# Three edits in one: shared stacks issued before the guest weights, an index order by fours, and two causal attentions worked in groups of two duos

## The reference, cut to what matters

```
h = rmsnorm(x)
A:   I[t,s] = sum_h w[t,h] * relu(qi[t,h] . ki[s])      # indexer, 8 heads
     keep the 128 best causal keys of each query, softmax over them, times va
B:   softmax(q.k/8 + c[t] - c[s], causal) v             # "forgetting" attention, 8 heads
x  = x + rmsnorm((sig(h Wma) * yA + sig(h Wmb) * yB) Wout), then a gated embedding
even layer: differential attention of 8 heads x 2 maps over 768 keys (256 context, 512 tokens),
            a short convolution, modulation of both layers from (silu(c) w_mod)
odd layer:  neighbourhood attention, Fourier mixing
```

## Time and profile before

| what | value |
|---|---|
| median of 3 runs | 1315.1 us (1314.51 to 1316.66) |
| profiled execution | 1319.82 us, its span 1317.9 us |
| PE busy | 1246.1 us, 95% |
| weight loads of PE | 999.3 us, 76% |
| DVE, ACT, POOL busy | 675.4, 632.7, 463.3 us |
| mean granted TensorE clock | 0.981 of full |
| moved by DMA | 140.33 MB, mean 106 GB/s |

### The profile page before, as it was taken

One profiled execution on the slowest core, in us unless ns is written; L12 is line 12 of the kernel. 1 busy time (PEld: TensorE's weight loads), 2 busy tenths in 40 slices (PEclk: granted clock), 3 DMA queues, 4 the chain that ended last, 5 costly groups with the idle time before them and its releaser, 6 DMA issues. The chain is left out here.

```text
span 1317.9 us, 19569 instructions
## 1 busy us (share of the span) xinstructions
PE 1246.1 (95%) x7148; PEld 999.3 (76%) x7148; DVE 675.4 (51%) x1293; ACT 632.7 (48%) x1355; POOL 463.3 (35%) x360
## 2 busy tenths in 40 slices
PE   7999999999999999899598989999999999999997
PEld 6877777776788788888476767788878788777785
DVE  4676966655315245547173637551834701555353
ACT  7544327654523366623264646552546422655533
POOL 5544434221444455512132323331452323222351
PEclk9999999999999999999798989999999999999999
DMA  6322541101322523501325341221234232221442
GB/s 230 134 72 70 187 160 65 65 33 49 128 97 95 193 96 106 197 1 65 113 94 182 116 168 59 93 75 65 96 112 146 85 115 86 67 94 65 161 133 91
DMA packets 28429, 140.33 MB, mean 106 GB/s; under 512 B 4304, under 2 KB 5712, under 8 KB 15728
## 3 DMA queue, kind: packets, MB, share of 16 engines
q1 hardware_dynamic: 21584, 117.72, 25.5%
q10 hardware_dynamic: 6752, 21.35, 4.9%
HBM read 122.74 MB, written 6.29 MB: 98 GB/s over the span
## 5 line engine op out<-in xcount | busy, mean ns | idle before, releaser
L1255 POOL TENSOR_TENSOR w_low<-w_raw,w_high 128x512 fp32r<-128x512 f32 x256 | 350.5, 1381 | 653.0 <-ACT w_high L1436 652.4
L1436 ACT CAST w_high<-w_raw 128x512 fp32r<-128x512 f32 x256 | 153.9, 621 | 258.5 <-PE psum L660 171.7
L660 PE MATMUL psum<-x_high,w_high 128*128 128x512 f32 x528 | 219.2, 415 | 3.7 <-DVE e_conv L2614 1.0
L660 PE MATMUL psum<-x_high,w_low 128*128 128x512 f32 x528 | 206.6, 391 | 0.0
L660 PE MATMUL psum<-x_low,w_high 128*128 128x512 f32 x528 | 206.2, 391 | 0.0
L660 PEld LDWEIGHTS psum<-x_high,w_high 128*128 128x128 f32 x528 | 99.7, 189 | 32.8 <-issue 10.1
L660 PEld LDWEIGHTS psum<-x_high,w_low 128*128 128x128 f32 x528 | 99.1, 188 | 21.6
L660 PEld LDWEIGHTS psum<-x_low,w_high 128*128 128x128 f32 x528 | 99.6, 189 | 16.6 <-issue 1.0
L2550 DVE TENSOR_REDUCE small<-psum 128x1 f32<-128x768 f32 (+1 forms) x96 | 70.0, 771 | 72.1 <-PE psum L1040 72.1
L660 PE MATMUL psum<-w_high,x_high 128*128 128x512 f32 x224 | 88.4, 395 | 0.9 <-POOL w_low L1255 0.6
L660 PE MATMUL psum<-w_high,x_low 128*128 128x512 f32 x224 | 87.3, 390 | 0.0
(11 more groups left out here) (484 smaller groups left out, 2862.0 us busy)
## 6 DMA issues: line engine op xcount, KB each, us to landing
w_raw<-stream SPq DMA_DIRECT2D x98, 1024.0 KB, 4.9
x_kept<-arena ACTq DMA_DIRECT2D x8, 512.0 KB, 3.7
arena<-x_kept ACTq DMA_DIRECT2D x8, 512.0 KB, 5.6
arena<-bias ACTq DMA_DIRECT2D x8, 512.0 KB, 3.9
q_masked<-e_q_high SPq DMA_DIRECT2D x24, 96.0 KB, 2.5
arena<-x SPq DMA_DIRECT2D x4, 512.0 KB, 5.2
arena<-x ACTq DMA_DIRECT2D x4, 512.0 KB, 5.0
arena<-ctx ACTq DMA_DIRECT2D x4, 512.0 KB, 4.4
```

Source lines behind the costliest of these rows:

```text
L660: mm = pe.matmul(o, l, r, start=(first and n == 0 and kind != "fc"), stop=(last and n == len(passes) - 1))
L1255: pool.tensor_tensor(PLACE[u][1], RAW[:, g % 2, u % 4, :], PLACE[u][0].bitcast(F32), ALU.subtract).then_inc(w_lo, 1)
L1436: act.copy(PLACE[u][0], RAW[:, g % 2, u % 4, :]).then_inc(w_hi, 1)
```

## The change

1. **Stacks and guests.** The stacks may be issued from the granule after `cb_0`'s on, and a modulation's granule counts as free one step later than before. Modulation parts of the even attention are now five, (0,4) to (1,2), after steps 2, 10, 18, 34 and 42, none after 26. Part (1,3) is a guest of `eo0` after its units 1 and 4, and is turned after the first tile of `eo1`. The order in SP's queue becomes: `cb_0`+`ub_0`, stack -1, first half of (0,4), second half, stack 1, `bb_0`+`cb_1`, both halves of (0,5), stack 10, `bb_1`+`ub_1`, first half of (1,0), stack 13 (before: stack -1 behind both halves of (0,4), stack 10 behind the first half of (1,0), stack 23 between the halves of (1,1)). ACT no longer rounds `n_k`'s first two units before the context's last norm.
2. **Index order.** `INDEX_SUMS` goes by groups of four (0, 2, 1, 3, then 4, 6, 5, 7 and so on), `ga`'s gate is multiplied one round of the selection earlier (n == 7 for 8).
3. **Causal attentions.** Every fourth step: transposes of step s-4 and a product piece first, then the values of two duos into one bank, then the scores of two duos into banks 0 to 3; on the other steps only transposes and a product piece. All transposes use bank 4. ACT copies values of two duos at once (16 copies of 256 columns for 32 of 128); exponentials, norms and copies come one step earlier in the lists of ACT and DVE.

```diff
-LATE_HOSTS = ("n_k", "ud")
-EVEN_MODS = [m for m in MODS if m not in MODS[:4] + MODS[10:]]
+GUEST_AT = {"eo0": (1, 4)}
+LATE_HOSTS = ("eo0", "n_k", "ud")
+EVEN_MODS = dict(zip((0, 1, 2, 4, 5), MODS[4:9]))
...
-        INDEX_SUMS = [6 * pr + n for pr in range(HEADS // 2) for n in (0, 2, 1, 3, 4, 5)]
+        INDEX_SUMS = [first + n for first in range(0, len(INDEX), 4) for n in (0, 2, 1, 3)]
...
-                accs = score_pair(keys, (s % 3, (s + 1) % 3), prep_of(name, pr), t, kh, kl, more=name == "b")
+                accs = score_pair(keys, (s % 4, s % 4 + 1), prep_of(name, pr), t, kh, kl, more=name == "b")
...
-                acc = open_bank(key, 3 + s % 2)
+                acc = open_bank(key, 4)
...
-            for s in range(len(BOTH) + 7):
-                if s >= 8 and s % 2 == 0:
-                    values_both((s - 8) // 2)
-                if s < len(BOTH) and s % 2 == 0:
-                    score_both(s)
+            for s in range(len(BOTH) + 5):
                 if 4 <= s < len(BOTH) + 4:
                     turn_both(s - 4)
                 if s < len(BOTH):
                     feed("ab", pieces, 1)
+                if s >= 8 and s % 4 == 0:
+                    values_both(s // 2 - 3)
+                if s < len(BOTH) and s % 4 == 0:
+                    score_both(s)
+                    score_both(s + 2)
...
-            by_tiles("eo1", mixed, gives_back=False)
+            by_tiles("eo1", mixed, lambda t: turn_due(), gives_back=False)
...
-                return min([s for s, mod in MOD_AFTER.items() if mod == granule[1]], default=len(EVEN))
+                return min([s + 1 for s, mod in MOD_AFTER.items() if mod == granule[1]], default=len(EVEN))
...
-                if g >= granule_of(UNITS["cb_1"][-1]):
+                if g > granule_of(UNITS["cb_0"][-1]):
...
-            for s in range(len(BOTH) + 8):
+            for s in range(len(BOTH) + 5):
...
-                if 2 <= s < len(BOTH) + 2:
-                    exps_both(s - 2)
-                if 5 <= s < len(BOTH) + 5:
-                    turned_out(*BOTH[s - 5])
-                if s >= 9 and s % 2:
-                    values_both((s - 9) // 2)
+                if 1 <= s < len(BOTH) + 1:
+                    exps_both(s - 1)
+                if 4 <= s < len(BOTH) + 4:
+                    turned_out(*BOTH[s - 4])
+                if s >= 8 and s % 4 == 0:
+                    values_both(s // 2 - 3)
...
             high(UNITS["eo1"][-1])
             mixed_out(0, range(ST))
+            guest_rows(GUEST["eo0"])
...
-            high(UNITS["n_k"][1])
             rms("x3_c", LT, lambda t: E_O[:, ST + t, :], context_summed, M_JUNK, c=ST, each=True)
...
-                if n == 8:
+                if n == 7:
                     gated("ga", GA)
...
-            for s in range(1, len(BOTH) + 5):
-                maxima_both(s - 1)
-                if 3 <= s < len(BOTH) + 3:
-                    name, i = BOTH[s - 3]
+            for s in range(len(BOTH) + 4):
+                if 2 <= s < len(BOTH) + 2:
+                    name, i = BOTH[s - 2]
                     norm(name)(i, ATT[name].tile(i))
-                if s >= 5:
-                    turned_out(*BOTH[s - 5])
+                maxima_both(s)
+                if s >= 4:
+                    turned_out(*BOTH[s - 4])
```

More of the change, by code:

```diff
@@ L66 @@
 HOSTS = ("ga", "gb", "vb", "mb0")
-LATE_HOSTS = ("n_k", "ud")
-EVEN_MODS = [m for m in MODS if m not in MODS[:4] + MODS[10:]]
-GUEST = {host: mod for host, mod in zip(HOSTS + LATE_HOSTS, MODS[:4] + MODS[10:])}
+LATE_HOSTS = ("eo0", "n_k", "ud")
+EVEN_MODS = dict(zip((0, 1, 2, 4, 5), MODS[4:9]))
+GUEST = {host: mod for host, mod in zip(HOSTS + LATE_HOSTS, MODS[:4] + MODS[9:])}
 UNITS = {}
@@ L84 @@
     _j, _rest = divmod(4 * _b - UNITS[SLIM[0]][0], 4)
-    if 0 <= _j < len(EVEN_MODS):
+    if _j in EVEN_MODS:
         GRANULES += [("m", EVEN_MODS[_j], half) for half in range(2)]
@@ L453, in build @@
         GRANULE_STEPS = 8
-        MOD_AFTER = {GRANULE_STEPS * j + 2: mod for j, mod in enumerate(EVEN_MODS)}
+        MOD_AFTER = {GRANULE_STEPS * j + 2: mod for j, mod in EVEN_MODS.items()}
         TURN_AFTER = {step + 2: mod for step, mod in MOD_AFTER.items() if mod[1] < 4}
         def even_units(s):
-            granules_in = (s - 5) // GRANULE_STEPS + 1
-            return min(fed["e"][2 * s - 1] + ROOM, UNITS[SLIM[0]][0] + 4 * granules_in + 3)
+            in_step, rest = divmod(s - 5, GRANULE_STEPS)
+            known = in_step + 1 if in_step in EVEN_MODS or in_step < 0 else in_step + 2
+            return min(fed["e"][2 * s - 1] + ROOM, UNITS[SLIM[0]][0] + 4 * known + 3)
         N_CONSTS = 3
@@ L771, in gemm @@
                     unit(chunk, k, x, c, part)
-                    if chunk in GUEST and k in (1, 5):
+                    if chunk in GUEST and k in GUEST_AT.get(chunk, (1, 5)):
                         modulate(*GUEST[chunk], int(k > 1))
@@ L920, in values_both @@
                 name, d = BOTH_DUOS[n]
[L921 to L924, removed]
+                if (name, d) == ("b", 1):
                     for kt in range(ST):
@@ L928, in values_both @@
                 acc = open_bank(key, 5)
-                for kt in range(t + 1):
+                for duo in (d - 1, d):
+                    pr, t = ATT[name].duos[duo]
                     for hh in range(2):
[L931 to L934, removed]
+                        consumed(pe, (name, "T", 2 * duo + hh, 0))
+                    own = slice(P * (duo % 2), P * (duo % 2) + P)
+                    for kt in range(t + 1):
+                        for hh in range(2):
+                            head = 2 * pr + hh
+                            v = A_VW[:, kt, 0:64] if name == "a" else A_VB[:, kt, 64 * head:64 * head + 64]
+                            mm = pe.matmul(acc[64 * hh:64 * hh + 64, own], v,
+                                           A_PT[:, 2 * (duo % 2) + hh, P * kt:P * kt + P], start=kt == 0, stop=kt == t)
                 fills_bank(mm, key)
@@ L1574, in _ @@
                 w = P * (t + 1)
-                if n % 6 == 0 and pr + 1 < HEADS // 2:
-                    prep_i(pr + 1)
+                if n % 6 == 0 and n // 6 + 1 < HEADS // 2:
+                    prep_i(n // 6 + 1)
                 if n >= 3:
@@ L1610, in turned_out @@
                 if d >= 2:
-                    filled(act, (name, "O", d - 2))
+                    filled(act, (name, "O", d - 2 | 1))
                 elif name == "b":
-                    filled(act, ("a", "O", len(ATT["a"].duos) - 2 + d))
+                    filled(act, ("a", "O", len(ATT["a"].duos) - 1))
                 n, key = a.keys(a.tile(i)), (name, "T", i, 0)
@@ L1643, in values_both @@
                 q = A_QA if name == "a" else A_QB
-                frees(act.copy(q[:, pr, P * t:P * t + P], ps[:, 0:P]), key)
+                frees(act.copy(q[:, pr, P * (t - 1):P * (t + 1)], ps[:, 0:2 * P]), key)
             def kept_raw(c):
@@ L2299, in gated @@
                     frees(dve.tensor_tensor(g[:, j, :], g[:, j, :], BANK[fills[(c, j)][0]][:, :], ALU.mult), (c, j))
[L2301 to L2304, removed]
             def modulation(layer, parts, rows=None):
@@ L2326, in modulation @@
                         consumed(dve, ("modT", layer, i))
-                    scale_up(layer)
+                    a, b = COL[f"npre{layer}"]
+                    link(dve.scalar_tensor_tensor(MC[:, layer, 8:16, :], MC[:, layer, 8:16, :], 1.0,
+                                                  COLS[:, a:b].unsqueeze(2).broadcast_to((P, 8, 2)), ALU.add, ALU.mult))
             link(dve.tensor_scalar(A_MASK[:, 0:P], square("causal"), -1.0, None, ALU.mult))
@@ L2356, in turned_out @@
                 if d >= 2:
-                    filled(dve, (name, "O", d - 2))
+                    filled(dve, (name, "O", d - 2 | 1))
                 elif name == "b":
-                    filled(dve, ("a", "O", len(ATT["a"].duos) - 2 + d))
+                    filled(dve, ("a", "O", len(ATT["a"].duos) - 1))
                 key = (name, "T", i, 0)
@@ L2395, in _ @@
             modulation(0, (1,))
-            for s in range(1, len(BOTH) + 5):
-                maxima_both(s - 1)
-                if 3 <= s < len(BOTH) + 3:
-                    name, i = BOTH[s - 3]
+            for s in range(len(BOTH) + 4):
+                if 2 <= s < len(BOTH) + 2:
+                    name, i = BOTH[s - 2]
                     norm(name)(i, ATT[name].tile(i))
-                if s >= 5:
-                    turned_out(*BOTH[s - 5])
+                maxima_both(s)
+                if s >= 4:
+                    turned_out(*BOTH[s - 4])
             for c, name, q, g, hi, lo in (("ga", "oa", A_QA, GA, BH, BL), ("gb", "ob", A_QB, GB, CHA, CLA)):
-                for d in range(len(ATT[name[1]].duos)):
+                for d in range(1, len(ATT[name[1]].duos), 2):
                     consumed(dve, (name[1], "O", d))
@@ L2637, in _ @@
```

(8 more changed lines are left out.)

## The result

The changed kernel takes 1296.9 us (median of 4 runs, 1294.9 to 1298.5), the kernel before 1315.9 in the same comparison (1314.5 to 1318.6). The ratio is 0.9845, 95% interval 0.9826 to 0.9864: faster by 19 us. The forecast was 1288, range 1279 to 1302: the direction and the range held, the gain of 27 was 8 too high.

A forecast was written before the change was run, and what follows sets the result against it. PE was taken as the bound, busy 1246.1 of 1317.9 us. Stacks 33.0, `eo1` -3.0, context norm +2.3, index +4.0 and attentions -9.1 sum to 27.2 off the 1315.1 median: 1288, range 1279 to 1302.

The forecast's parts named there:

- Part 1, stacks: Even attention: earlier stacks and no modulation after step 26 remove waits and low clock, 35.5 us, net 33.0.
- Moving (1,3): Even attention after step 26: no modulation left, so 5.85 us of load wait and 2.9 + 0.1 of low clock go.
- `eo1`: First tile of `eo1`: its loads land later and POOL's eight low parts finish late; PE loses about 3.0 us, bounds 0 and 6.
- Context norm: Context's last norm: DVE's two sums get faster, PE's wait shrinks about 1.5 us, half the clock fall counted; +2.3, bounds 0 and 3.6.
- Index: Index scores and `gate_a`: new order frees banks and gates earlier, ending waits of 2.9 and 1.1 us; +4.0, bounds 2.5 and 4.
- Part 3, the attentions: Causal attentions: waits on the single transpose bank's copies outweigh regrouping gains; -9.1 us, bounds -5.6 and -11.5.
- shape changes: Causal attentions: fewer switches between matmul shapes per two duos, saving 3.2 us.
- The single bank costs nothing: Rival, causal attentions: prompt copies remove the waits, so the stage gains 7.6 us; 1271, or 1280 if half vanish; chance 0.15.
- the start isn't freed: Rival, even attention's start: something else holds the stacks, so 18.9 us stay; 1307; chance 0.08.
- The clock falls in the attentions: Rival, causal attentions: short waits lower the clock in every group, 16 x 1.5 = 24 us; 1312, half of them 1300; chance 0.10.
- my term of 3.0 for the low clock there: Even attention, behind the load wait after step 26: 2.9 + 0.1 us of low clock expected to go.

The follow-up runs named there:

- SP's order alone: Kernel before with only the new order of SP's queue, all six modulations staying in the even attention: 1292.5 against 1316.0 us, ratio 0.9804.
- the last experiment: Changed kernel with transposes alternating between banks 4 and 5, plus the first half of a finished `ma` chunk copied one step earlier by ACT: 1275.9 us, ratio 0.9686.
- two banks: Changed kernel with transposes taking turns between banks 4 and 5, a group's values using the one free between: 1276.7 us, ratio 0.9699.
- the copy ahead of the next maximum: Changed kernel with the copy of a transposed block placed before the next maximum in DVE's list instead of behind it: 1290.2 us, ratio 0.9796.
- attentions-alone kernel: Kernel before with only the causal attentions' new order and single transpose bank, stacks and index as before: 1332.9 against 1316.1 us, ratio 1.0122.
- the cut in the kernel before: Kernel before with POOL's low parts of the attention weights cut to 8 of 512 columns; single run, attention stage 122.4 us against 123.6.
- both edits: Changed kernel with transposes in banks 4 and 5 and DVE's copy of a transposed block ahead of the next maximum: 1277.9 us, ratio 0.9700.

## Why the prediction was right, and where it was off

*Part 1, stacks: held.* The text has 26.6 for the waits of the start and of step 13, less 2.5 for new ones: 24.1; SP's order alone measured 23.5. Moving (1,3): 8.85 of wait and low clock less 3.0 at `eo1`, 5.9; measured 4.7. Together 30.0 against 28.2. In the traces the even attention's stretch gained 33.6 and the next one lost 1.9, but the profiled execution of before had more time at a low clock than others (below).

*`eo1`: held.* POOL finishes eight low parts one after the other, and the first tile waits for each of the last five; 1.9 us in the table and 2.3 against the run with (1,3) left in place, for 3.0 forecast.

*Context norm: its mechanism half wrong.* 1.3 us on average in the traces, nothing in the medians, against 2.3. The sums got faster as told; that POOL's part would hit DVE's next low part instead and take back 1.3 of the 1.7 was not foreseen. What is left is about the clock fall behind the wait, of which the prediction counted half.

*Index: held,* 4.0 against 4.0 between the two traces, to the tenth by luck: with the old order the attentions begin at 202.6 to 205.3 us in four traces, with the new one at 198.1 to 199.2 in ten, on average 5.1 earlier. The waits named (2.9 and 1.1) are gone. No run changes the index order alone.

*Part 3, the attentions: the step that failed.* The mechanism was right: the single bank, waits on copies at the transposes, "some 15 to 20 us in all" (15.8 by the profile). The sum of -9.1 with bounds of -5.6 and -11.5 was not: alone it measured -16.8, in the traces -14.5, or -15.4 at the same clock. That is the whole error of the forecast: 9.1 less 17 to 18 is the 8 to 9 us by which the medians missed 1288. The prediction had two workings. By hand: 17.6 + 0.3 + 2.9 of waits, less the 3.5 of old waits and 3.2 of shape changes, is 14.1, close to what the traces show. The walk of both orders through their lists gave 130.7 less 121.5 = 9.2, and I took it although the two differed by 5, and the text gives no reason for the gap. The old order's 121.5 was close to its measured 122.7; the new one's 130.7 was 7.4 short. Two runs say what it left out. DVE's norms take longer beside POOL: 3.4 us of the new stage, and 0.3 of the old one at the same clock. ACT's copies of finished sums hold PE's next product (1.9 us in the last experiment, with two banks; by start-to-start times some 0.7 with one, which no run of its own shows). The rest, about 3 us, stays open.

The start-to-start times show how large the waits are. A transpose behind a product starts 0.232 us after it when nothing waits. In the old order 30 of these take 7.3 us, so 0.3 of wait; in the new one 46 take 31.7, so 21.0 of wait, where the waits view shows 15.8: it counts idle time only from the modelled end of the product. With two banks the same 46 take 12.1.

The order without its waits seems to have saved more than the 3.2 put down for shape changes. By the same start-to-start times all waits in the new stage add up to about 25 us and in the old one to about 5, so without them it went from some 118 to 113 us. That is an estimate by subtraction; no run shows which change of shape gave it.

*The rivals.* "The single bank costs nothing" and "the start isn't freed" are refuted by the two-bank run and by SP's order alone. (The 7.6 in the first doesn't follow from the prediction's own terms, 3.2 + 3.5 = 6.7; with two banks the stage gained 2.2.) "The clock falls in the attentions" did not come: with 25 waits of up to 1.8 us the stage runs at a granted clock of 1.00, that is 2.4 GHz:

```profile
200.00:250.00 50.00, 41.51 (x308) 28.63 (x306) 31.47 (x114) 29.61 (x84) 13.58 (x11) 1.00 0.12 43
250.00:300.00 50.00, 45.55 (x357) 32.40 (x357) 28.99 (x88) 27.14 (x78) 11.00 (x9) 1.00 0.07 22
300.00:350.00 50.00, 45.66 (x325) 32.81 (x325) 32.55 (x72) 25.61 (x63) 11.81 (x9) 1.00 0.23 75
```

Nor does it fall in the stage of four other traces with the single bank; a fifth (the copy ahead of the next maximum) has one fall, 1.7 us. The old order has one fall in two of its four traces. The rule of the Trainium skill that stood beside that rival ("TensorE: Matmul & The Clock Gate", "A second HAM failure mode: psum-queue depth-cycling") finds no case of a fall in every group here.

## What to carry to other kernels

When two workings of the same term differ, the range must hold both: take neither as the value before the gap is explained. When work is regrouped, count the buffers between two engines first: a second bank was worth more (20 us) than the regrouping itself (2). A transfer without conditions of its own behind one that must wait is the cheapest thing to look for in a queue: two lines of order gave 23 us.

## What the runs showed of the hardware that I had not expected

*Much the same wait costs more low clock in one execution than in another.* PE's wait for the load after step 26 was 5.85 us in the kernel before, with 0.71 granted in the 10 us behind it. In the attentions-alone kernel it was 5.06 (ending at 795.03), and the 10 us behind it had 0.83, which is 1.7 us lost instead of 3.0. Its windows:

```profile
790.00:800.00 10.00, 4.97 (x38) 2.91 (x39) 1.31 (x4) 2.06 (x8) 0.28 (x1) 0.83 0.80 282
800.00:810.00 10.00, 10.00 (x67) 8.66 (x66) 5.29 (x8) 6.15 (x17) 1.26 (x2) 1.00 0.11 45
```

The stretch of 187.1 us in the profiled execution of before (between the matmuls that stand at 773 and 960) is 183.9 and 183.6 in two other kernels in which the edits do not touch it (attentions alone, and the cut in the kernel before). So some 3 us of the difference between the traces (23) and the medians (19) is this execution's own (0.8 of it a longer wait, the rest the clock), and my term of 3.0 for the low clock there counted what not every run has. Behind shorter waits a fall can be missing altogether. With two banks and with both edits PE's waits are alike just before 550 (2.2 and 2.3 us for one, 2.1 for another):

```profile
540.00:550.00 10.00, 7.76 (x67) 7.56 (x66) 5.99 (x10) 5.22 (x11) 5.63 (x4) 1.00 0.96 341
```

```profile
540.00:550.00 10.00, 7.76 (x53) 7.76 (x54) 6.21 (x9) 5.13 (x11) 4.55 (x4) 0.83 0.98 383
```

The first is the two banks alone, at full clock; the second has both edits and 0.83, and again 0.83 from 660 to 670 where the first has 1.00. From the end of the attentions to the same matmul of the even attention (at about 740) the one takes 418.9 us and the other 421.6.

*The meeting of DVE and POOL recurs.* The schedule of the attentions repeats every eight steps (17 us here), and POOL's work with it. So a norm that meets a low part meets it again in every period: 1.18, 1.25 and 1.19 us at 222.6, 239.5 and 256.5. With two banks it does too, every 14 us: 1.18, 1.25 and 1.19 at 220.0, 234.4 and 248.2. The old order has its own meetings (its norms take 29.5 us, 26.3 with the cut), but they cost its stage only 0.3 us.
